# Moving the weight buffers from 64 to 256 bytes off the 2 KB grid of the operands

## What is computed

```python
h = x @ w_in                      # each mixer, 3072 to 8000 columns in all
y @ w_out
h = x @ w_up                      # 1024 x 5632, twice; ffn_in of block 2 as well
(jax.nn.silu(g) * u) @ w_down     # 2816 x 1024, three times
```

## Time and profile before

| | |
|---|---|
| median of 3 executions | 2798.62 us (2794.9 to 2827.63) |
| the profiled execution, its own time | 2813.04 us |
| its span, first to last instruction | 2811.2 us |
| PE busy | 2650.1 us, 94% |
| PEld busy | 2437.3 us, 87% |
| DVE busy | 1463.9 us, 52% |
| ACT busy | 1234.7 us, 44% |
| mean granted clock of TensorE | 0.985 |

### The profile page before, as it was taken

How to read it: one execution, slowest core, us unless ns; L and a number is a source line. 1 busy time by engine, 2 the same in 40 slices (tenths; PEclk the granted TensorE clock), 3 DMA queues, 4 the chain that set the end, 5 groups by cost and what they waited for, 6 DMA issues and landing times.

```text
span 2811.2 us, 51084 instructions
## 1 busy us (share of the span) xinstructions
PE 2650.1 (94%) x20916; PEld 2437.3 (87%) x20916; DVE 1463.9 (52%) x2506; ACT 1234.7 (44%) x2032; POOL 114.4 (4%) x177
## 2 busy tenths in 40 slices
PE   7998999999998699999989999989989998999998
PEld 7985899999997399999979776779956986899998
DVE  3223476553524766655467888852475343433333
ACT  3335353432425734342364877752475234333321
POOL 0000000000000000000001233300000000000000
PEclk9999999999999999999999999999999999999999
DMA  6420032223331013223344655532211321223232
GB/s 181 117 75 0 31 98 90 97 95 100 103 107 60 1 61 105 90 95 115 98 164 140 200 184 190 195 105 92 90 38 65 101 98 38 76 98 97 97 105 68
DMA packets 74702, 278.34 MB, mean 99 GB/s; under 512 B 9642, under 2 KB 9674, under 8 KB 74048
## 3 DMA queue, kind: packets, MB, share of 16 engines
q1 hardware_dynamic: 60816, 217.42, 23.2%
q0 software_dynamic: 13744, 58.88, 7.2%
HBM read 267.03 MB, written 9.24 MB: 98 GB/s over the span
## 4 chain that ended last, share of the span: by engine, by line
PE 75%; DVE 14%; ACT 7%; issue 3%; DMA 1%; SPq 0%; DVEq 0%; ACTq 0%
PE acc L338 63%; PE acc L369 2%; DVE big L1618 2%; DVE res_tmp L1911 2%; PE ps L813 1%; DMA w_raw<-in_stream 1%; DVE w_lo L319 1%; PE ps L369 1%; PE acc L1467 1%; ACT L285 1%; DVE res_tmp L1905 1%; DVE big L2214 1%; PE ps L453 1%; DVE big L1276 1%; ACT res_tmp L1882 1%
## 5 line engine op out<-in xcount | busy, mean ns | idle before, releaser
L338 PE MATMUL acc<-x_split,w_hi 128*128 128x256 f32 x7968 | 1257.9, 280 | 20.3 <-DVE x_split L1363 12.0
L338 PEld LDWEIGHTS acc<-x_split,w_hi 128*128 128x128 f32 x7968 | 1076.7, 190 | 24.6 <-issue 16.8
L319 DVE TENSOR_TENSOR w_lo<-w_raw,w_hi 128x1024 fp32r<-128x1024 f32 x405 | 494.3, 1221 | 606.9 <-ACT w_hi L313 606.9
L338 PE MATMUL acc<-x_split,w_lo 128*128 128x256 f32 x3984 | 788.8, 280 | 0.0
L313 ACT ACTIVATE w_hi<-w_raw 128x1024 fp32r<-128x1024 f32 x405 | 426.3, 1054 | 581.0 <-PE acc L338 528.1
L338 PEld LDWEIGHTS acc<-x_split,w_lo 128*128 128x128 f32 x3984 | 610.1, 190 | 0.0
L338 PE MATMUL acc<-big_r,w_hi 128*128 128x256 f32 x3560 | 563.4, 281 | 7.7 <-DVE big_r L2267 3.4
L338 PEld LDWEIGHTS acc<-big_r,w_hi 128*128 128x128 f32 x3560 | 482.6, 190 | 10.3 <-issue 4.1
L338 PE MATMUL acc<-big_r,w_lo 128*128 128x256 f32 x1780 | 353.6, 280 | 0.0
L338 PEld LDWEIGHTS acc<-big_r,w_lo 128*128 128x128 f32 x1780 | 272.8, 189 | 0.0
L958 ACT ACTIVATE res_tmp<-acc,par 128x512 f32<-128x512 f32 x84 | 64.9, 772 | 150.6 <-PE acc L338 146.0
(11 more groups left out here) (301 smaller groups left out, 2677.1 us busy)
## 6 DMA issues: line engine op xcount, KB each, us to landing
w_raw<-in_stream SPq DMA_DIRECT2D x405, 512.0 KB, 3.5
res_tmp<-scratch_rows POOLq DMA_DIRECT2D x96, 320.0 KB, 5.3
big<-scratch_rows POOLq DMA_DIRECT2D x32, 320.0 KB, 5.5
scratch_bias<-res_tmp POOLq DMA_DIRECT2D x1, 2560.0 KB, 56.6
res_tmp<-in_x SPq DMA_DIRECT2D x2, 1024.0 KB, 7.6
res_tmp<-scratch_bias POOLq DMA_DIRECT2D x8, 256.0 KB, 4.4
scratch_x<-res_tmp POOLq DMA_DIRECT2D x1, 2048.0 KB, 8.0
scratch_kv<-big POOLq DMA_DIRECT2D x1, 2048.0 KB, 9.5
```

The costliest lines, as they stand in the source:

```text
L319: dve.tensor_tensor(w_lo[:, u.slot], w_raw[:, u.slot], w_hi[:, u.slot].bitcast(F32), ALU.subtract).then_inc(lo_done, 1)
L338: mm = pe.matmul(a[:, h], w, AR[:, x + k, h], start=(k == 0 and w is wh and x == hi and h.start == 0), stop=(k == total - 1 and w is wl), ...
```

## The change

One number: the arena's room gets 64 floats more than the slots need, where it got 16. The slots keep their addresses, since they are placed at `base`. All that is allocated behind the room moves up by 192 bytes: `w_raw`, `w_hi`, `w_lo`, `par`, `const` and `small`. No instruction is added, removed or moved.

```diff
-        ctx.enter_context(nc.sbuf_tensor("arena_room", [P, N_SLOTS * S + 16], F32))
+        ctx.enter_context(nc.sbuf_tensor("arena_room", [P, N_SLOTS * S + 64], F32))
```

## The result

The changed kernel takes 2881.05 us (2880.67 to 2882.68, four executions) where the kernel before takes 2807.3 (2794.9 to 2827.63, four): a ratio of 1.0274, 95% interval 1.0237 to 1.0312. The profiled execution took 2881.0 us with a span of 2879.2, which is 68.0 us more than the 2811.2 of before. Beside the length, the spread is new: 2 us in place of 33.

A forecast was written before the change was run, and what follows sets the result against it. The step between L338's product matmuls, 1763 us of the chain, was taken to bound the kernel. With the short step throughout, 2813.0 − 37.9 (L338) − 2 (L369 and L1467) = 2773 us; range 2720 to 2855.

The forecast's parts named there:

- What bounds the kernel: PE busy in 94% of the span; the step between L338's product matmuls sets the pace for 1763 us of 2811.2.
- short rhythm: Step of 113.3 ns between L338's products, against 117.7 in the long one; holding it throughout had chance 0.33, 2773 us.
- the value after: Step forecast for all L338 products in the changed kernel: 113.3 ns.
- 37.9 us go: Gain in L338 if its 1013.4 us of long pieces drop from 117.7 to 113.3 ns a step.
- The floor: Lowest step thought possible for L338: 110.3 or 107.7 ns from plain fp32 matmuls, gaining 83.5 or 123 us.
- a step below the short one: Rival: L338's products go below 113.3 ns, to 110.3 ns, 2730 us, at the lowest bound 2690; chance 0.20.
- worse than the long rhythm: Rival: mean step of L338's products about 118.6 ns or more, slower by over 2% from 2855 us on; chance 0.10.
- the long rhythm everywhere: Rival: L338's 749 us of short pieces turn long, costing 29.1 + 2 us, 2844 us; chance 0.10.
- The range: Forecast whole-kernel time from 2720 us, taking in the 110.3 ns case, to 2855, taking in every L338 piece long.
- the last case: Rival beyond the upper end: L338's mean step from about 118.6 ns on, time above 2855 us; chance 0.10.
- The minor terms: Splits at 1.05 and 1.22 us and loads at 3.5 us stay hidden; `const`, `par`, `small` have little to gain.
- The draw of the rhythm: L338's step is drawn anew when other matmuls interrupt the products, then stays; it does not change in mid-stream.

The follow-up runs named there:

- e1: Changed kernel with the slots' base also 192 bytes higher, so weights again 64 bytes off the slots' grid: 2803.12 us, ratio 1.0006 to the kernel before.
- e2: Kernel before with 48 unused floats ahead of `par`, so only `par`, `const` and `small` move by 192 bytes: 2804.93 us, ratio 1.0002.
- e10: Kernel before, offset 64 bytes, with `product_tile` streaming 512 columns per weight load instead of 2 x 256: 2828.04 us, ratio 1.0063.
- e11: Changed kernel, offset 256 bytes, with `product_tile` streaming 512 columns per weight load: 2780.04 us, ratio 0.9901 to the kernel before.
- e17: Repeat in more executions of the kernel with 512 columns per load at 256 bytes: 2775.73 us, ratio 0.9901 to the kernel before.
- e9: Kernel before with 48 unused floats ahead of `w_lo`, so `w_lo` lies at 256 bytes, `w_raw` and `w_hi` at 64: 2845.63 us, ratio 1.0134.

## Why the prediction was wrong

**What bounds the kernel** was right. The 1763 us of L338, split into 1013 us of long and 749 us of short pieces, carried the whole change: with the measured step these pieces give 64.1 of the 68.0 us, and L369 and L1467 the rest. That the offset acts on these very products is shown too: e1 and e2 leave the distance between the slots and the weight buffers, the step does not depend on what ACT, DVE and the DMAs do (120 ns while they work and while they don't), and in e10 and e11 the offset still moves the step while the load has slack. With nothing but the distance changed, the step goes from 113.3 to 120.0 ns at 256 columns and from 226.7 to 233.3 at 512.

**The step that failed** is the value after: "I take the short rhythm, 113.3 ns, as the value after". The reason given was that these operands are seen to hold it for 355 us on end, with both reads at their shortest. That row was taken at the offset of 64 bytes, and so it could say what 64 bytes allow, and nothing of 256. The short rhythm depends on the offset: of the eight distances modulo 256 bytes, only 64 and 192 showed it over whole stages, and at 256 every product of L338 took 120.0 ns. In the sum the term "37.9 us go" became 64.1 us that come.

**The floor** was misread with it. The prediction compared 113.3 ns with 110.3 and 107.7 of other matmuls and gave 0.20 to a step below the short one. No offset went below 113.3. Whether anything could still go from the short rhythm stays open: by the estimate above it has 113.3 - 106.7 = 6.6 ns beside its columns, one half of the 13.3 at 256 bytes, and no run takes that apart. The 107.7 is half a step of plain fp32: what is measured is that its columns take twice the time of those of fp32r at 256 bytes (213.1 ns against 106.7 for 256 of them), not that it makes two passes. The 110.3 ns of L671 was also misread. It is a mean with one step of 139 ns in it, and the other 30 steps are 109 or 110. Nor did `const` at its new distance change this row, 3.69 us before and 3.68 now:

```profile
191.26 3.68 PE L671 MATMUL ps<-const,big 128*128 128x128 f32 x32 [0.87 <-ACT big L635]
```

**The rival that came true** was "worse than the long rhythm", with a chance of 0.10 and a mean step from 118.6 ns on. The sign was right, a further loss in the matmuls of L338: the step was 120.0 ns, 2.3 ns on top of the long one, and so 68 us came. What makes it longer was not shown. The rival "the long rhythm everywhere" ended at 2844; the chip ended above it. "Nothing in the trace shows such a step" was true, and it was used as evidence against one, though the trace has a single offset.

**The range** ended at 2855 because the last case was left out. Both directions of an unseen address relation deserved the same weight: the trace of before bounded what the old offset does, and the offset was what changed.

**The minor terms** held: the splits stayed at 1.05 and 1.22 us, the loads at 3.5 us from issue to landing, and `const` and `par` cost nothing (e2). In up0, 1669 matmuls came where 1767 were forecast. That the spread of the kernel before is the share of the long rhythm fits, since at 256 bytes, where every stage has one step, the executions lie within 2 us. It is not shown, for only one execution has a trace, and e17 spreads by 10 us with one step of 226.7 ns in L338.

**The draw of the rhythm** was told too narrowly. In the kernel before up0 begins in the short rhythm and turns into the long one at 396.84 us, in the middle of its products. No other matmul comes between, only a pause: the last product of the short rhythm began at 396.50, and the next one 0.35 us later. In the trace:

```profile
396.39 0.39 PE L338 MATMUL acc<-x_split,w_lo 128*128 128x256 f32 x2
396.84 0.73 PE L338 MATMUL acc<-x_split,w_hi 128*128 128x256 f32 x4
```

**What stays open** is why a distance costs what it costs. A period of 256 bytes agrees with both pairs tried, and the price depends on the width of the moving read and on the loads beside it (e9, 117.8 ns for all six). That the distance alone counts, and not the two addresses, rests on one pair of kernels, the one before and e1. No run shows what makes the distance count, and none what makes a stage at 64 bytes fall into the one rhythm or the other.

## What to carry to other kernels

Where TensorE streams against weight loads without a gap, divide a stretch by its count of matmuls. Two different steps at the same shapes and the same clock were the sign here that the place of the operands mattered. Then sweep the distance between the stationary and the moving buffers in steps of 32 bytes up to 256, on the chip, and do it again after any change of the moving width: here the best offset at 256 columns lay with the worst at 512. And do not infer from one offset's trace what another offset does, neither the sign nor the floor.

## What the hardware showed that was not expected

- The distance between the stationary and the moving operand in SBUF changes the step of fp32r matmuls: 113.3 to 120.0 ns at 256 columns and 226.7 to 233.4 at 512, with no instruction changed between the offsets of one width.
- Rhythms hold for hundreds of us, and several can come at the same addresses: 113.3 and 117.8 ns at 64 bytes, 116.7 and 117.8 at 224, 118.7 and 120.0 at 128. They turned where other matmuls had come between, and in the kernel before after a pause of 0.35 us without any.
- At 256 bytes, 256 more columns for each load take 106.7 ns (226.7 - 120.0), half of the 213.1 of plain fp32 (428.8 - 215.7). By that rate, an estimate, 13.3 ns are left for a load, although at 512 columns PEld stands idle for 39 ns a load.
- With w_hi at 64 and w_lo at 256 bytes there is one rhythm for all, at 117.8 ns, no mean of the two.
